# Output projection of an encoder layer: nine of twelve residual tiles turned on VectorE in 32x32 blocks and placed through DRAM, instead of turned on TensorE

## The reference, cut to what matters

```python
D_MODEL = 1024; SEQ = 512; DEC_SEQ = 1024; D_FF = 4 * D_MODEL      # 1536 tokens in two sequences

def encoder_layer(x, ...):
    ...
    a = block_swept_gqa(q, k, v)
    p = multiscale_pool(u, w_pool, pool_scale)
    x = x + jnp.concatenate([a, p], axis=-1) @ w_out    # the output projection and the residual
    h2 = rmsnorm(x, norm2_g)                            # x / sqrt(mean(x^2) + eps) * g
    x = x + jnp.square(jax.nn.relu(h2 @ w_up)) @ w_down
    return x
```

## Time and profile before

| | |
|---|---|
| median of 3 runs | 1484.53 us (1484.30 to 1484.99) |
| the profiled execution | 1483.54 us, of which 1481.8 us lie between its first and last instruction |
| PE busy | 1471.5 us of 1481.8 |
| DVE, ACT, POOL busy | 1042.6, 705.7, 401.1 us |
| granted TensorE clock | 1.000 of full speed |
| the stage that is changed | from 411 us to about 557 us of the span |

### The profile page before, as it was taken

How to read it: one execution, slowest core, us unless ns; L and a number is a source line. 1 busy time by engine, 2 the same in 40 slices (tenths; PEclk the granted TensorE clock), 3 DMA queues, 4 the chain that set the end, 5 groups by cost and what they waited for, 6 DMA issues and landing times.

```text
span 1481.8 us, 23179 instructions
## 1 busy us (share of the span) xinstructions
PE 1471.5 (99%) x7884; PEld 1312.3 (89%) x7884; DVE 1042.6 (70%) x1301; ACT 705.7 (48%) x1195; POOL 401.1 (27%) x347
## 2 busy tenths in 40 slices
PE   9999999999999999999999999999999999999999
PEld 8999878888888889999999999999888888888887
DVE  6766799999856675544454545448888878878875
ACT  6223399999833344545454545456322322323220
POOL 3467599888910010000000000001320311311300
PEclk9999999999999999999999999999999999999999
DMA  8654331000246639343334323347744343343434
GB/s 262 154 121 112 98 90 24 20 11 14 83 146 250 219 113 413 132 146 125 129 113 157 134 109 134 137 155 291 264 157 153 104 149 122 125 156 105 137 99 183
DMA packets 89066, 209.10 MB, mean 141 GB/s; under 512 B 8240, under 2 KB 27568, under 8 KB 88880
## 3 DMA queue, kind: packets, MB, share of 16 engines
q1 hardware_dynamic: 86816, 197.27, 39.9%
q10 hardware_dynamic: 2192, 11.08, 1.8%
HBM read 129.93 MB, written 71.57 MB: 136 GB/s over the span
## 4 chain that ended last, share of the span: by engine, by line
PE 93%; DVE 2%; ACT 2%; POOL 1%; issue 1%; DMA 0%; ACTq 0%; POOLq 0%; DVEq 0%
PE ps L871 24%; PE ps L873 24%; PE ps L872 24%; PE ps L1134 6%; PE ps L1016 4%; PE ps L1144 3%; PE ps L1031 2%; PE ps L998 2%; PE ps L1032 2%; PE ps L1000 2%; ACT prob L1351 1%; PE ps L1154 1%; POOL prob L2414 0%; DVE pTlo L1744 0%; DVE nmax L1806 0%
## 5 line engine op out<-in xcount | busy, mean ns | idle before, releaser
L871 PE MATMUL ps<-h,wuhi 128*128 128x384 f32 (+1 forms) x904 | 301.5, 334 | 0.2 <-issue 0.2
L873 PE MATMUL ps<-h,wulo 128*128 128x384 f32 (+1 forms) x904 | 301.2, 333 | 0.0
L872 PE MATMUL ps<-h,wuhi 128*128 128x384 f32 (+1 forms) x904 | 301.2, 333 | 0.0
L871 PE MATMUL ps<-wdhi,hidhi 128*128 128x512 f32 x672 | 261.6, 389 | 0.0
L873 PE MATMUL ps<-wdhi,hidlo 128*128 128x512 f32 x672 | 261.6, 389 | 0.0
L872 PE MATMUL ps<-wdlo,hidhi 128*128 128x512 f32 x672 | 261.5, 389 | 0.0
L2220 DVE TENSOR_TENSOR yacc<-yacc,ps 128x1024 f32<-128x1024 f32 x167 | 203.2, 1217 | 78.1 <-PE ps L873 78.1
L1270 ACT ACTIVATE hidhi<-hin 128x1024 fp32r<-128x1024 f32 (+1 forms) x72 | 86.8, 1205 | 300.7 <-PE ps L873 292.8
L2134 DVE TENSOR_TENSOR u<-u,ps 128x384 f32<-128x384 f32 x96 | 53.1, 553 | 181.7 <-PE ps L873 181.7
L871 PEld LDWEIGHTS ps<-h,wuhi 128*128 128x128 f32 x904 | 169.7, 188 | 0.7 <-issue 0.4
L872 PEld LDWEIGHTS ps<-h,wuhi 128*128 128x128 f32 x904 | 169.8, 188 | 0.0
(11 more groups left out here) (217 smaller groups left out, 2804.2 us busy)
## 6 DMA issues: line engine op xcount, KB each, us to landing
hd<-hout SPq DMA_DIRECT2D x64, 384.0 KB, 3.2
hin<-hd SPq DMA_DIRECT2D x48, 512.0 KB, 3.7
hd<-hout SPq DMA_DIRECT2D x32, 576.0 KB, 2.8
hin<-hd SPq DMA_DIRECT2D x24, 768.0 KB, 4.4
wuraw<-in_w_up SPq DMA_DIRECT2D x17, 1024.0 KB, 6.0
wdraw<-in_w_down SPq DMA_DIRECT2D x8, 2048.0 KB, 9.4
h<-h2d ACTq DMA_DIRECT2D x7, 1536.0 KB, 11.6
x2in<-in_x SPq DMA_DIRECT2D x12, 512.0 KB, 3.3
```

Source lines behind the costliest of these rows:

```text
L871: pe.matmul(out, w_hi, m_hi, start=start, stop=False, skip_group_check=resumed)
L872: pe.matmul(out, w_hi, m_lo, start=False, stop=False, skip_group_check=resumed)
L873: return pe.matmul(out, w_lo, m_hi, start=False, stop=stop, skip_group_check=resumed)
```

## The change

For the first nine tiles (`TURNED = TT - 3`) PE no longer transposes. `scale_x2` writes to two free PSUM banks, and DVE turns the 32x32 blocks from there into `x2turn` (4 KB a partition, in the place of `xs2`). ACT issues four stores of 32 partitions each to DRAM (`spill_x2`, 128 KB each), waits for them to land, and issues one load of 512 KB (`place_x2`) into one of three buffers `x2T`. `hi_h2` and `lo_h2` read from there. The last three tiles are transposed on PE as before. The order on DVE and ACT changes for rounds 1 to 9, as does the place of `store_h2` among SP's transfers. ACT's squares go to PSUM as well. Some semaphores are merged, which changes no order.

```diff
+        x2T = [at("x2T0", C + 57344, [4, KT, 32]), at("x2T1", ...), at("x2T2", ...)]
+        x2turn = at("x2turn", C + 16384, [4, KT, 32])
+        x2d = nc.dram_tensor("x2d", [TT, 4, 32, 4, 256], F32).ap()
...
+        TURNED = TT - 3
+        PLACES = (0, 1, 2, 0, 1, 2, 0, 1, 0)
+        def turned_x2(p):
+            return (x2_placed, 16 * p + 16) if p < TURNED else (xT2_done, p - TURNED + 1)
+        def junk_banks():
+            return psw[:, 2048:3072]
...
@@ SP, for p in range(TT)
-                if p in (2, 4, 6):
-                    store_h2((p - 2) // 2)
                 store_x2(p)
                 if p + 2 < TT:
                     load_x2(p + 2)
+                if p in (2, 4, 6):
+                    store_h2((p - 2) // 2)
@@ PE, project_out(p)
-                if p:
+                if p > TURNED:
                     transpose_x2(p - 1)
@@ ACT
             def square_x2(p):
                 if p:
                     act.wait_ge(ms2_done, p)
                     act.wait_ge(ss2_done, p)
-                act.activation(junk2[:], x2in[:, p % 2], ACT.Square, scale=D ** -0.5, accum_out=ssx[:]
+                    act.wait_ge(x2T_done, min(p, TURNED))
+                act.activation(junk_banks(), x2in[:, p % 2], ACT.Square, scale=D ** -0.5, accum_out=ssx[:]
...
+            def spill_x2(p):
+                act.wait_ge(x2T_done, p + 1)
+                for b in range(4):
+                    act.dma_start(x2d[p].rearrange("q c b n -> b c q n")[b],
+                                  x2turn[b * 32:b * 32 + 32].rearrange("c q k t -> c q (k t)")).then_inc(x2_spilled, 16)
+            def place_x2(p):
+                last = max((i for i in range(p) if PLACES[i] == PLACES[p]), default=None)
+                act.wait_ge(x2_spilled, 64 * (p + 1))
+                if last is not None:
...                     (waits until DVE has read tile `last` out of the buffer)
+                act.dma_start(x2T[PLACES[p]][:].rearrange("p b k t -> p (b k t)"),
+                              x2d[p].rearrange("q c b n -> (q c) (b n)")).then_inc(x2_placed, 16)
...
             square_x2(0)
+            split_c(2)
+            spill_x2(0)
+            place_x2(0)
             for p in range(1, TT):
-                if p + 1 < TT:
-                    split_c(p + 1)
+                if p <= TURNED:
+                    square_x2(p)
+                    if p + 2 < TT:
+                        split_c(p + 2)
+                    if p < TURNED:
+                        spill_x2(p)
+                    hi_h2(p - 1)
+                    if p < TURNED:
+                        place_x2(p)
+                elif p + 1 < TT:
                     hi_h2(p - 1)
@@ DVE
             def scale_x2(p):
                 dve.wait_ge(rs2_done, p + 1)
-                if p:
-                    dve.wait_ge(xT2_done, p)
-                dve.scalar_tensor_tensor(xs2[:], x2in[:, p % 2], rsx[:, 0:1], g2b[:], ALU.mult, ALU.mult
+                if p < TURNED:
+                    dve.wait_ge(x2T_done, p)
...
+                dve.scalar_tensor_tensor(junk_banks() if p < TURNED else xs2[:], x2in[:, p % 2], rsx[:, 0:1], g2b[:],
+                                         ALU.mult, ALU.mult).then_inc(xs2_done, 1)
+            def turn_x2(p):
+                dve.wait_ge(xs2_done, p + 1)
+                dve.wait_ge(x2_spilled, 64 * p)
+                dve.transpose(x2turn[:], junk_banks().rearrange("p (k q c) -> p q k c", k=KT, q=4)).then_inc(x2T_done, 1)
...
             residual(0)
+            split_c(2)
             scale_x2(0)
+            turn_x2(0)
             for p in range(1, TT):
-                if p + 1 < TT:
-                    split_c(p + 1)
-                if p < TT - 2:
+                if p <= TURNED:
+                    residual(p)
+                    if p + 2 < TT:
+                        split_c(p + 2)
+                    scale_x2(p)
+                    if p < TURNED:
+                        turn_x2(p)
                     lo_h2(p - 1)
-                    residual(p)
-                    scale_x2(p)
```

More of the change, by code:

```diff
@@ L486, in wu_place, with blocked, h2_psum, h2_bank @@
             return (wuhi6, wulo6) if isinstance(w, int) and (w, o) == (0, 6) else (wuhi[o], wulo[o])
-        def h2_bank(q, b):
+        TURNED = TT - 3
+        PLACES = (0, 1, 2, 0, 1, 2, 0, 1, 0)
+        def blocked(tile):
+            return tile.rearrange("p k (b t) -> p k b t", b=4)
+        def h2_psum(q, b):
             bank = b - 2 if b > 1 and q == TT // 2 - 1 else 4 + b
             return ps[:, bank].rearrange("p (k c) -> p k c", k=4)
+        def h2_bank(q, b):
+            if 2 * q + b // 2 < TURNED:
+                return x2T[PLACES[2 * q + b // 2]][:].rearrange("p b k t -> p k b t")[:, b % 2 * 4:b % 2 * 4 + 4]
+            return blocked(h2_psum(q, b))
+        def turned_x2(p):
+            return (x2_placed, 16 * p + 16) if p < TURNED else (xT2_done, p - TURNED + 1)
+        def junk_banks():
+            return psw[:, 2048:3072]
         def h2_staged(q, a):
@@ L498, in h2_half @@
             if q < QT_TILES:
-                return h2_staged(q, 2 * o + low).bitcast(F32R)
-            return h2[1][o][:, low, q - QT_TILES]
+                return blocked(h2_staged(q, 2 * o + low).bitcast(F32R))
+            return blocked(h2[1][o][:, low, q - QT_TILES])
         def h2_full(q, o):
             if q < QT_TILES:
-                return h2_staged(q, 2 * o + 1)
-            return h2raw[o][:, q - QT_TILES]
+                return blocked(h2_staged(q, 2 * o + 1))
+            return blocked(h2raw[o][:, q - QT_TILES])
         def up_bank(par, o):
@@ L1160, in transpose_last @@
                 for k in range(4):
-                    mm = pe.transpose(h2_bank(TT // 2 - 1, 2)[:, k], xs2[:, k * P:(k + 1) * P], ident[:])
+                    mm = pe.transpose(h2_psum(TT // 2 - 1, 2)[:, k], xs2[:, k * P:(k + 1) * P], ident[:])
                 mm.then_inc(xT2_half, 1)
@@ L1164, in transpose_last @@
                 for k in range(4):
-                    mm = pe.transpose(h2_bank(TT // 2 - 1, 3)[:, k], xs2[:, (k + 4) * P:(k + 5) * P], ident[:])
+                    mm = pe.transpose(h2_psum(TT // 2 - 1, 3)[:, k], xs2[:, (k + 4) * P:(k + 5) * P], ident[:])
                 mm.then_inc(xT2_done, 1)
@@ L1688, in down_chunk @@
                                 hi_wd(n + 1, 1 - z, o)
+            def spill_x2(p):
[7 more added lines that the diff above has]
+                if last is not None:
+                    if last % 2:
+                        act.wait_ge(h2_lo, SLOTS * (last // 2 + 1))
+                    else:
+                        act.wait_ge(h2_sum, 4 * (last // 2 + 1))
+                act.dma_start(x2T[PLACES[p]][:].rearrange("p b k t -> p (b k t)"),
+                              x2d[p].rearrange("q c b n -> (q c) (b n)")).then_inc(x2_placed, 16)
             split_c(1)
@@ L1706, in _ @@
                     square_last()
-                else:
+                elif p > TURNED:
                     square_x2(p)
@@ L2552, in _ @@
                 norm_x2(p)
-            norm_halves(1, TT, ms2_done, ss2_done)
+            pool.wait_ge(ss_half, 1)
+            pool.tensor_tensor(msx[:], ssx[:], epsx[:], ALU.add).then_inc(ms2_done, 1)
+            pool.wait_ge(ms2_done, TT)
+            pool.wait_ge(ss2_done, TT)
+            pool.tensor_tensor(msx_b[:], msx[:], ssx_b[:], ALU.add).then_inc(ms2_done, 1)
+            pool.wait_ge(ms2_done, TT + 1)
             pool.wait_ge(xs2_done, TT - 1)
```

59 lines of the change are left out of this document (26 added, 33 removed).

## The result

The changed kernel takes **1501.12 us** (median of 4 runs, 1500.92 to 1501.94) against 1484.54 before (4 runs): ratio 1.0112, 95% interval 1.0095 to 1.013. It is slower by 16.6 us, where the prediction had +6.0 and a range that ended at 1499. The direction was right, the size too small.

What follows compares the result with a forecast made beforehand. PE, busy 1471.5 of 1481.8 us, was taken to bound the kernel, DVE's chain after the change. Structure 2.3, landing 2.1 and clock 1.6 made +6.0, so 1489.5 against the profiled execution and 1490.5 as median; range 1483 to 1499.

Steps and rivals of the forecast that it cites:

- What is removed, 8.1 us at most: On PE: nine turns of 0.90 us each go, which is all the change can gain.
- The structure, +2.3: DVE's chain becomes longer than PE's was; tile 9's transposes begin at 537.5 instead of 535.2, 2.3 us longer.
- rival B: Posed with the experiments, no chance given: the new order on DVE and ACT is the loss, whatever the DMA does.
- laid out: DVE's rounds, from one residual to the next: 11.2 us in odd rounds and 13.4 in even ones.
- The turn, 1.3 us: DVE's turn of a tile, 1024 elements in runs of 32: 1.3 us, bounds 1.26 and 2.14.
- The rival of the slow turn: PSUM source or stride makes DVE's turn cost 2.14 us: 6.7 more over eight rounds, 1497; chance 0.13.
- The issues: ACT's four stores take 1.78 us to issue, as on SP, ahead of its copies in odd rounds.
- The landing, +2.1: ACT's wait in `place_x2` for its stores, beside an h2 store: 0.7 us in each of rounds 3, 5 and 7.
- The clock, +1.6: PE's clock may fall after the 7.5 us wait before tile 9's transposes: 0 to 4.5 us, taken as 1.6.
- stores that land late: ACT's stores land beyond 5 us behind the h2 stores, each us more costing 3: 1495 to 1502; chance 0.12.
- turns of a packet each: The DMA engines take the queues that have work in turn, a packet at a time; no size given.

Runs made afterwards that it cites:

- kernel 11: The changed kernel with ACT's copies ahead of its square, the load back one round later, and h2 stores of 2 of 14 planes: 1477.31 us.
- kernel 8: The changed kernel with one store and four loads, ACT's copies ahead of its square, and only tiles 0 to 2 turned by DVE: 1482.13 us.
- kernel 1: The changed kernel with SP's three h2 stores writing only 2 of the 14 planes, wrong data, read for time alone: 1490.67 us.
- kernel 6: The changed kernel with each tile stored to DRAM in one store and rearranged by four loads of 32 partitions: 1502.55 us.
- kernels 2: The changed kernel with ACT's two copies into chi ahead of its square in each round: 1495.96 us.
- kernel 7: The changed kernel with one store and four loads per tile, and ACT's copies of the next operand ahead of its square: 1493.42 us.
- kernel 9: The changed kernel with only a quarter of each tile after the first stored through ACT's queue, h2 stores in full: 1495.95 us.

## Why the prediction was right in direction and too small

- **What is removed, 8.1 us at most.** Right: 7.0 us in kernel 11, 2.5 of 2.7 in kernel 8.
- **The structure, +2.3.** Right. This part of the loss is rival B's; as an explanation of the rest B falls with kernels 1 and 11. Rounds 1 and 2 were 11.46 and 13.30 for 11.2 and 13.4. With small h2 stores (kernel 1) the eight rounds sum to 99.95 us, 98.4 predicted, and the 1.6 more are rounds 4 and 8, with the landing in them. DVE did wait 2.26 us for ACT's copies in each round whose square was on time. Most of PE's wait moved to `clo`, from projection 6 on, since DVE fell behind sooner than laid out.
- **The turn, 1.3 us.** 1.249. The rival of the slow turn fell, with the scaling into PSUM at 1.29 for 1.28 as well. The Trainium skill (Vector Engine (DVE) Microarchitecture Reference, 3.8) has the transpose sustain one element a cycle in each lane. This row agrees: it lasts hardly longer than DVE's sum over as many elements (1.22).
- **The issues.** This is the step that failed: "Four such stores took SP 1.78 us to issue", taken for every round. Unloaded it held: 1.8 to 2.35. In rounds 3, 5 and 7 they took 4.78, 4.98 and 5.01, 9.4 us more in all than laid out, and these rounds were 8.9 us longer. The sum had nothing for it: I had put the loaded DMA engines into the landing only.
- **The landing, +2.1.** Near: rounds 4, 6 and 8 were 0.96, 1.25 and 0.62 us longer than laid out, 2.8 together. In round 3 the load back followed the last issue by 3.64 us and the square came 0.5 behind it, 0.9 later than it was due. The term is right only for this order, though: in kernel 6, with three of four issues gone, the wait for the landing, and the four loads behind it, cost as much as both.
- **The clock, +1.6.** 2.1 us behind tile 9's transposes. The size was near and the mechanism right: the granted clock of the stretch around them is 0.69, a mixture of the two levels (the row below). The longer matmul groups before it (5.53 for 3.79) cost nothing of their own, since DVE's chain set the time there.
- **Sum.** In the profiled execution: 2.3 laid out, 8.9 behind the issues, 2.8 for the landing and 0.2 in rounds 1 and 2 make 14.2, for the 14.1 us measured in the stage; with 2.1 for the clock that is 16.2. The medians give 1501.1 - 1484.5 = 16.6, of which 10.4 go with the h2 stores' bytes and 6.2 stay in kernel 1. That kernel 1 measures the forecast's 1490.5 is no accident: it has what the forecast reckoned with, the structure, a little landing and the clock, without the long issues. The rival "stores that land late" had 1495 to 1502 at 0.12, and the measured time lies in it. The stores did land late, 6.2 us from their issue (median of the four of round 3), but for much of that time ACT was still issuing; behind the last issue the load followed within 3.3 to 3.6 us, which by the rival's own price costs 1 to 2 us in all. Its cause, the h2 stores, is what happened; its path is not, and that the time lies in its range is in part luck.

## What to carry to other kernels

An issue is an instruction of its engine, and its length is not a constant: price it from a row in which the DMA engines are as full as they will be at the new place, and ask what stands behind it. Shortening the issues or moving them to another engine moved the same delay elsewhere. Putting ACT's copies ahead of what waits gave 5 to 8 us back (kernels 2 and 7), not enough. Only less traffic in that stretch, or turning only the tiles outside it, came out faster than before. Before a detour through DRAM goes into a loop, lay the loop's other transfers over it round by round, and use it only where they leave room.

## What the runs showed of the hardware that was not expected

- The first issue on an idle queue takes 0.34 us even with the engines 98% busy (kernel 6, 465.60, in the stretch from 459 to 472 us). Four in a row under that load take 4.1 to 5.7 us together, with a quarter of the bytes too (kernel 9). SP's own issue behind its h2 stores took 3.54 us (460.34), and 0.42 at 474.23, when they had drained. The Trainium skill (DMA: Bandwidth & Descriptors, Rules for kernel authors) says that spreading transfers over more issuing engines gives no bandwidth and only saves issue time. The traces agree on the bandwidth: SP's queue alone filled the engines before the change (share 1.03 from 474 to 482 us), and with ACT's beside it they are as full (0.99). Of the issue time the second engine saved less here: ACT's queue paid 4.8 us for 2.2. Why the later issues wait is not settled.
- Sharing is not even. From 466.3 to 471.1 us q10 had 75 packets moved beside 927 of q1. The prediction reckoned with turns of a packet each; these counts don't show that, and why is open.
- PE's clock. Two stretches of the changed kernel by windows, the granted clock third from the end:

```profile
492.00:497.00 5.00, 4.83 (x14) 3.83 (x15) 2.57 (x3) 0.00 (x0) 0.00 (x0) 0.66 1.04 382
```

```profile
546.00:557.00 11.00, 6.57 (x25) 5.49 (x25) 6.46 (x9) 6.54 (x13) 0.74 (x2) 0.69 0.50 191
```

Waits of 1.1 to 1.3 us left the group behind at 3.92 to 3.96 us. Behind 2.02 and 2.14 us it took 5.53, behind 4.02 us 6.25. But a wait of 2.40 us in kernel 9 and one of 3.25 in kernel 7 were followed by 3.92 and 3.93. So these rows don't tie the fall to the length of the wait alone, and what else it needs stays open.
